# A two-layer decoder trunk on one core: the first 512 tokens of the second projection are normed and turned in the mixing phase's sample part, with two chunk buffers and key-value products per head

## The reference, cut to what matters

```python
for l in range(DEPTH):                                   # 2 layers
    mod = silu(c) @ w_ada[l] + b_ada[l]                  # conditioning: 1024 -> 3072
    shift, scale, gate = split(mod, 3)
    h = rms_norm(x, g_pre[l]) * (1 + scale) + shift
    y = mixer_ab(h) if l == 0 else mixer_c(h)            # projection in, mixing, projection out
    x = x + gate * rms_norm(y, g_post[l])
# in mixer_ab, per chunk and head (8 heads, key width 64, value width 128):
#   o = (q k^T, masked) v + q S ;  S = S * decay + k^T v
```

## Time and profile before

| | us |
|---|---|
| median of 3 runs | 2918.32 |
| lowest, highest | 2914.44, 2925.43 |
| time of the profiled execution | 2930.07 |
| its span, first to last instruction | 2928.3 |
| mean granted TensorE clock | 0.934 of full speed |

### The profile page before, as it was taken

The page is one execution under the profiler, slowest core; times in us unless marked ns, Lnnn a source line. Parts: engine busy times, 40 slices in busy tenths (PEclk is TensorE's granted clock), DMA queues, the critical chain, the costliest instruction groups (busy, mean ns, idle before and its releaser), DMA issues. The chain is left out here.

```text
span 2928.3 us, 54792 instructions
## 1 busy us (share of the span) xinstructions
PE 2645.6 (90%) x21216; PEld 1572.3 (54%) x21280; DVE 1386.1 (47%) x3146; ACT 932.6 (32%) x2711; POOL 768.8 (26%) x844
## 2 busy tenths in 40 slices
PE   7989999997599999398899999984899999999997
PEld 2434444444456653244444444453788887878783
DVE  3221212110477744486262644633566656666635
ACT  2532222222111110343131321213454554545431
POOL 1430101000311100254000010001655656465531
PEclk9999999998799988699999999997899999999977
DMA  7350212012564432355121111115431323222212
GB/s 261 112 150 31 87 37 76 29 69 78 164 220 143 143 123 68 95 164 147 38 72 54 62 58 48 51 43 129 136 89 59 97 61 94 74 81 79 62 37 72
DMA packets 264259, 270.28 MB, mean 92 GB/s; under 512 B 32126, under 2 KB 199438, under 8 KB 264015
## 3 DMA queue, kind: packets, MB, share of 16 engines
q1 hardware_dynamic: 185948, 219.50, 23.1%
q10 hardware_dynamic: 78112, 47.87, 6.1%
HBM read 179.96 MB, written 87.36 MB: 91 GB/s over the span
## 5 line engine op out<-in xcount | busy, mean ns | idle before, releaser
L518 PE MATMUL inc_b<-inc_h,inc_w_hi 128*128 128x512 bf16 (+2 forms) x1906 | 481.2, 347 | 30.1 <-DVE inc_h L462 17.2
L518 PE MATMUL inab_b<-inab_wt,inab_h 128*128 128x512 f16 (+1 forms) x1632 | 362.0, 385 | 13.0 <-POOL inab_wt L498 13.0
L518 PE MATMUL inc_b<-inc_h,inc_w_lo 128*128 128x512 bf16 (+1 forms) x926 | 301.9, 345 | 0.0
L518 PEld LDWEIGHTS inc_b<-inc_h,inc_w_hi 128*128 128x128 f16 x1920 | 170.6, 100 | 210.9 <-DVE inc_h L462 16.3
L518 PEld LDWEIGHTS inab_b<-inab_wt,inab_h 128*128 128x128 bf16 (+3 forms) x1632 | 162.6, 100 | 210.6 <-issue 26.5
L518 PE MATMUL inab_b<-inab_h,inab_wc_hi 128*128 128x512 f16 (+4 forms) x712 | 183.3, 352 | 10.7 <-DVE inab_h L462 8.0
L518 PE MATMUL inc_b<-inc_w_hi,inc_h 128*128 128x512 f16 (+3 forms) x816 | 176.4, 314 | 15.0 <-POOL inc_w_lo L498 14.3
L1777 DVE SCALAR_TENSOR_TENSOR inc_acc<-inc_ub,inc_taps,inc_acc 128x512 f32<-128x512 f32 (+1 forms) x240 | 167.5, 698 | 8.6
L1692 ACT ACTIVATE inc_ub<-inc_b 128x512 f32<-128x512 f32 x96 | 57.3, 597 | 313.1 <-PE inc_b L518 309.0
L518 PEld LDWEIGHTS inc_b<-inc_h,inc_w_lo 128*128 128x128 f16 x960 | 94.3, 100 | 93.2 <-issue 4.4
L768 ACT ACTIVATE inab_vz<-inab_b 128x512 f32<-128x512 f32 (+1 forms) x68 | 40.6, 597 | 289.6 <-PE inab_b L518 286.2
(11 more groups left out here) (415 smaller groups left out, 5534.9 us busy)
## 6 DMA issues: line engine op xcount, KB each, us to landing
tmp_qkv<-inc_so SPq DMA_DIRECT2D x96, 256.0 KB, 2.0
mixc_qkv<-tmp_qkv SPq DMA_DIRECT2D x15, 1536.0 KB, 7.7
inc_stage<-in_w_in_c ACTq DMA_DIRECT2D x32, 512.0 KB, 4.6
inab_wt<-in_w_ada SPq DMA_DIRECT2D x6, 2048.0 KB, 10.7
inab_stage<-in_w_in_ab ACTq DMA_DIRECT2D x24, 512.0 KB, 4.1
mixab_cw<-in_w_ada ACTq DMA_DIRECT2D x6, 2048.0 KB, 9.3
inab_x<-in_x_prompt SPq DMA_DIRECT2D x16, 512.0 KB, 4.7
tmp_v<-inab_vz SPq DMA_DIRECT2D x32, 256.0 KB, 3.6
```

The costliest lines, as they stand in the source:

```text
L518: last = nc.tensor.matmul(dst, lhs(a, k), rhs(b, k), start=(k == 0 and i == 0), stop=(k == KT - 1 and i == len(PASSES) - 1))
```

## The change

What is changed: (a) in mix_ab `key_values` makes one product for each head, with 64 columns of keys, so that the result lies in one bank, `kv1`, as DVE wants it; `update` is one addition; `turn_k` waits for `ktok_ready` in place of `state_ready`, and `key_values` waits for `state_ready`. The sample's products are made in the same way, into two banks. (b) `Cond` has two chunk buffers in this phase in place of three. (c) A new class `Early` loads, squares, norms, turns and stores (into `raw_next`, which lives through both phases) the first four tiles of x in the sample part. (d) Phase in_c leaves its `Prep` work for block 0 out, and uses `first_low`, `first_high` and `first_rest`, which wait for nothing of the conditioning; ACT's copy of the taps comes behind `first_low`, and the lower parts of the first weights go from DVE to POOL.

```diff
 class Cond: ... RING = 3  ->  self.ring = len(w); in mix_ab two buffers
+class Early:
+    def load(self, eng, t):
+        wait(eng, self.xnd, t)
+        eng.dma_start(self.x, self.src[t * P:(t + 1) * P, :]).then_inc(self.x_in, 16)
+    def square(self, act, t):
+        act.wait_ge(self.x_in, 16 * (t + 1))
+        wait(act, self.tr, t)
+        act.activation(self.xn, self.x, ACT.Square, accum_out=self.ss[:, t:t + 1]).then_inc(self.sq, 1)
+    def rstd(self, pool, t):                    # two operations on POOL, as in Prep
+    def norm(self, act, t):
+        act.wait_ge(self.rsd, t + 1)
+        act.activation(self.xn, self.x, ACT.Copy, scale=self.rs[:, t:t + 1]).then_inc(self.xnd, 1)
+    def turn(self, pe, t):
+        pe.wait_ge(self.xnd, t + 1)
+        wait(pe, self.done, t)
+        for k in range(KT):                     # 8 transposes into banks be, bo
+            last = self.nc.tensor.transpose(...)
+        last.then_inc(self.tr, 1)
+    def take(self, act, t):
+        act.wait_ge(self.tr, t + 1)
+        for i in range(2):
+            last = act.activation(self.raw[:, 4 * i:4 * i + 4, t * P:(t + 1) * P], self.banks[i]..., ACT.Copy)
+        last.then_inc(self.done, 1)
 phase_mix_ab, ACT:
-        for n in range(Cond.RING):
+        for n in range(2):
             cond.load(act, n)
...
-        cond.load(act, 3)
+        cond.load(act, 2)
...
         ktok_copy(nt, NS)
-        cond.load(act, 4)
+        early.load(act, 0)
+        cond.load(act, 3)
...
+        cond.load(act, 4)
+        early.square(act, 0)
+        oT_copy(nt, NS)
         cond.load(act, 5)
-        oT_copy(nt, NS)
+        def first_tile(t):
+            if t:
+                early.square(act, t)
+            early.norm(act, t)
+            if t + 1 < TPB:
+                early.load(act, t + 1)
+            early.take(act, t)
+        first_tile(0)
+        first_tile(1)
         cond.take(act)
         cond.gates(act)
+        first_tile(2)
+        first_tile(3)
 phase_mix_ab, DVE:
-            for e in range(2):
-                rows = slice(e * DKA, (e + 1) * DKA)
-                for i in range(2):
-                    kv = kvbank[i][:].rearrange("p (g e d) -> p g e d", g=2, e=2)[rows, :, e, :]
-                    last = dve.tensor_tensor(U[rows, 2 * i:2 * i + 2, :], S1[rows, 2 * i:2 * i + 2, :], kv, ALU.add)
-            chain.link(last)
+            chain.link(dve.tensor_tensor(U[:], S1[:], kv1[:].rearrange("p (g d) -> p g d", g=PAIRS), ALU.add))
 phase_mix_ab, PE:
-            wait(pe, state_ready, t)                  # turn_k
+            wait(pe, ktok_ready, t)
...
             pe.wait_ge(ktok_ready, t + 1)             # key_values
+            wait(pe, state_ready, t)
             for p in range(PAIRS):
-                last = nc.tensor.matmul(kvbank[p // 2][:, (p % 2) * 256:(p % 2 + 1) * 256], ktok[:, p, :],
-                                        v[par][:, 2 * p:2 * p + 2, :], start=True, stop=True)
+                for e in range(2):
+                    rows = slice(e * DKA, (e + 1) * DKA)
+                    last = nc.tensor.matmul(kv1[rows, p * DV:(p + 1) * DV], ktok[:, p, rows], v[par][:, 2 * p + e, :], start=True, stop=True)
...
             if p == 2:
                 cond.turn(pe)
                 cond.spread_gates(pe)
+            early.turn(pe, p)
 phase_in_c:
-        for t in range(2):
-            prep.load(sp, t, t, P)
+        prep.first_tiles_done(sp)
...
+        weights.hi(act, 0)
+        prep.first_low(act, None, m_a, m_v, first_hi)
         act.wait_ge(taps_turned, 1)
...
-        for t in range(TPB):
-            prep.norm(dve, t, t % 2, P)
-            prep.modulate_high(dve, t)
-            weights.lo(dve, t)
-        prep.copy(dve, TPB, mm, 0, BLK)
+        prep.first_high(dve, None, m_v, first_hi, first_lo_p, first_lo_v)
```

More of the change, by code:

```diff
@@ L204, in __init__ @@
         self.ident, self.sel, self.sel_s = ident, sel, sel_s
-        self.psM, self.psT, self.psG = psM, psT, psG
+        self.psM, self.psT, self.psG, self.ring = psM, psT, psG, len(w)
         s = ph.sem
-        self.w_in = [s(f"c_w_in{i}") for i in range(self.RING)]
+        self.w_in = [s(f"c_w_in{i}") for i in range(self.ring)]
         self.small_in, self.mm, self.chain, self.mod_ready = s("c_small_in"), s("c_mm"), s("c_chain"), s("c_mod_ready")
@@ L582, in phase_in_ab @@
     c9, c_silu = vz_flat[0:C9, 0:D], vz_flat[0:C9, D:2 * D]
[L583 removed]
+    ring = [w_room[:, i * 4096:(i + 1) * 4096].rearrange("p (k n) -> p k n", k=KT) for i in range(3)]
     cond = Cond(nc, ph, 0, io, modT, ring, w_room[0:C9, 12288:12288 + 3 * D], w_room[0:C9, 15360:15360 + D], r_flat[0:C9, 0:D],
@@ L1069, in phase_mix_ab @@
     cT_in, vm_ready = s("cT_in"), s("vm_ready")
-    ring = [ph.sb(f"cw{i}", [P, KT, 512]) for i in range(Cond.RING)]
+    ring = [ph.sb(f"cw{i}", [P, KT, 512]) for i in range(2)]
+    exn = ph.sb("exn", [P, D])
     mod = ph.sb("mod", [C9, 3 * D])
@@ L1182, in _ @@
         rstd(nt, NS)
+        for t in range(TPB):
+            early.rstd(pool, t)
         fin.rstd(pool, nt, NS)
@@ L1374, in _ @@
             dve.wait_ge(kv_done, nt + p + 1)
-            sv = [kv0, kv1, b_even, b_odd]
-            for i in range(4):
-                for e in range(2):
-                    rows = slice(e * DKA, (e + 1) * DKA)
-                    kv = sv[i][:].rearrange("p (s e d) -> p s e d", s=2, e=2)[rows, :, e, :]
-                    last = dve.tensor_tensor(Ss[p][rows, 2 * i:2 * i + 2, :], Ss[p][rows, 2 * i:2 * i + 2, :], kv, ALU.add)
+            for i, kv in enumerate((kv0, kv1)):
+                part = Ss[p][:, 4 * i:4 * i + 4, :]
+                last = dve.tensor_tensor(part, part, kv[:].rearrange("p (s d) -> p s d", s=4), ALU.add)
             chain.link(last)
@@ L1504, in _ @@
             pe.wait_ge(state_ready, nt + p)
-            sv = [kv0, kv1, b_even, b_odd]
-            for i in range(4):
-                last = nc.tensor.matmul(sv[i][:], ktok[0:NS, p, :], vm[p % 2][:, 2 * i:2 * i + 2, :], start=True, stop=True)
+            for i, kv in enumerate((kv0, kv1)):
+                for e in range(2):
+                    rows = slice(e * DKA, (e + 1) * DKA)
+                    last = nc.tensor.matmul(kv[rows, :], ktok[0:NS, p, rows], vm[p % 2][:, 4 * i:4 * i + 4, e * DV:(e + 1) * DV], start=True, stop=True)
             last.then_inc(kv_done, 1)
@@ L1584, in _ @@
         sp.dma_start(alog[:, 1, :], io["dt_bias_c"].unsqueeze(0).to_broadcast([P, H])).then_inc(small_in, 16)
-        for t in range(TPB):
-            sp.wait_ge(prep.xnd, t + 1)
-            prep.load(sp, t + 2, t % 2, P)
+        for t in range(TPB, TPB + 2):
+            prep.load(sp, t, t % 2, P)
         for i in range(2):
@@ L1637, in _ @@
         pool.wait_ge(prep.half_set, 1)
-        for t in range(TPB):
-            if t == 0:
-                prep.rstd(pool, 0, 0, P)
-            if t + 1 < TPB:
-                prep.rstd(pool, t + 1, (t + 1) % 2, P)
-            prep.split_lo(pool, t, t * P, P)
-        pool.wait_ge(weights.lo_done, AHEAD)
+        weights.lo(pool, 0)
+        prep.first_rest(pool, first_hi, first_lo_p)
+        for u in range(1, AHEAD):
+            weights.lo(pool, u)
         for g in range(G):
@@ L1667, in _ @@
         last.then_inc(taps_ready, 1)
-        for t in range(TPB):
-            if t == 0:
-                prep.first_square(act, 0)
-            if t + 1 < TPB:
-                prep.first_square(act, t + 1)
-            prep.modulate_low(act, t)
-            prep.split_hi(act, t, t + 1, t * P, P, 0)
-            weights.hi(act, t)
+        for u in range(1, AHEAD):
+            weights.hi(act, u)
         act.wait_ge(zero, 1)
@@ L1831, in _ @@
         pe.wait_ge(taps_ready, 1)
-        for t in range(TPB):
-            prep.turn(pe, t, P)
         seen = set()
```

53 lines of the change are left out of this document (38 added, 15 removed).

## The result

| | before | changed |
|---|---|---|
| median, us | 2921.88 (4 runs) | 2884.32 (4 runs) |
| lowest, highest | 2914.44, 2927.62 | 2880.74, 2890.29 |
| span of the profiled execution | 2928.3 | 2879.0 |

(Three of the four runs of before are those shown ahead of the prediction.) The ratio of the changed kernel to the kernel before is 0.9878, with a 95% interval of 0.9848 to 0.9908: about 36 us less. The prediction was 2869.3 us, 15 us lower.

The account below looks back on a forecast made before the run. PE, busy nine tenths of the span, bounds the kernel, so its gaps and needless work count. Terms -34.5 (in_c start), -18 (tile loop), +3.5 (sample part) sum to -49.0: median 2918.32 to 2869.3 us, range 2857 to 2886.

Parts of the forecast that it names:

- Start of in_c: Phase in_c: block 0's serial chain goes, so the first product starts at 1194.1, not 1228.66; 34.5 us less.
- rival B: Late transfers: sample-part chunk 8 to 15 us, or weight units hold in_c's first products by 5; 2877 to 2884; chance 0.18.
- I price this at nothing: Start of in_c: one weight unit ready instead of four costs nothing; some 5 us if units came late.
- Tile loop: mix_ab: shorter key-value products and no state wait cut the period from 18.35 to 17.34 us; 18 us less in all.
- Rivals A: Key-value products: column halves don't overlap; 4.3 us less loop gain, 6.6 us more in sample part; 2880; chance 0.15.
- C: Key-value products: each pass holds the array alone, weight load uncovered; total about 2920, no change; with the like, chance 0.05.
- if the stall stayed, it would be 14: mix_ab loop: gain of 14 us, not 18, if the 3.8 us stall at tiles 3 and 4 remained.
- Two chunk buffers: mix_ab: conditioning chunk n waits for chunk n-2; priced at 0, or 15 us with the slowest landing.
- Sample part: mix_ab's sample part: early x work outweighs shorter key-value products, so the sample's projection starts 3.5 us later.
- rival D: PE's granted clock stays low longer because of gaps in the sample part; +6 us, 2875; chance 0.12.
- the gap ahead of L1066: Sample part, sign of the forecast: PE stands idle ahead of L1066 for x tiles 2 and 3.
- the three that would have made the account wrong: Single-file `128*64` products at over 0.2 us; L231 waiting for `mixab_cw`; L518's product waiting for `inc_w_lo` in first four products.

Follow-up runs that it names:

- Experiment 1: Changed kernel, but ACT gives the signal for in_c's first product ahead of the upper parts of weight units 1 to 3; 2875.89 us, ratio 0.9843 to before.
- experiment 3: Changed kernel, but the loop's key transposes (`turn_k`) wait for `state_ready` again, as in the kernel before; 2885.39 us, one run.
- experiment 2: Kernel before with the per-head key-value products alone (loop and sample part), three chunk buffers, no early x work; 2903.40 us, ratio 0.9944.
- experiment 4: Changed kernel, but conditioning chunk 1 is loaded at tile 9 of the loop, not right behind chunk 0 at tile 3; 2881.04 us, ratio 0.9857 to before.
- sample order: Changed kernel, but ACT squares and norms x tile 2 ahead of `cond.take` and the gates; 2876.47 us, ratio 0.9846 to before.
- h first: Changed kernel with Experiment 1's edit, and weight unit 0 converted in the middle of making h, not ahead; 2872.18 us, ratio 0.9836 to before.
- all: Changed kernel with early signal, h first, chunks apart, sample order, and first half waiting only for the first gate operation; 2861.23 us, ratio 0.9796 to before.

## Why the prediction came out as it did

**Start of in_c: the step that failed.** "So h is ready at 1178.89 + 4.5 + 1.04 + 9.65 = 1194.1, and the first product starts there rather than at 1228.66." The first half is right, 15.2 us against 14.5. The second supposed that PE waits for h and its weights alone. PE's first product also waits for `evac`, which says that its bank is free; at the phase's start no bank is in use, and ACT gives the signal once for all of them. It gave it behind `weights.hi` of units 1 to 3. In the kernel before this cost nothing, as the same units were converted while h was made; now h overtakes them. Experiment 1 moved this signal, with the one given beside it, and nothing else, and in_c took 7.3 us less; missing were 34.5 - 27.6 = 6.9. That the weights might be late (rival B's second half) was the right place with the wrong wait: not PE's need of the units, but a signal queued behind them. That the measured 2884 us lie at the edge of B's 2877 to 2884 is luck. "I price this at nothing" is right for the units themselves: the first products never waited for them.

**Tile loop: right in the mechanism, 3 us too much.** The period was forecast at 17.34 us and is 17.25; the sixteen narrow products at 1.0 and are 1.09; the wait went to `mixab_y` as said. Rivals A and C are out: the column halves do run beside each other. One sentence of the working is wrong, though the sum did not use it: "DVE's shorter `update` moves nothing by itself". It looked at the norm behind `update` alone, but the state is written ahead of the norm and released PE's key transposes; with this wait kept, the shorter `update` was worth 0.84 us a tile (experiment 3). What was wrong in the sum is "which supposes that with two chunk loads in place of three (4 MB of traffic, not 6) the 3.8 us stall is gone". It is still 4.5 us, and between 3.8 and 4.8 in all traces with two chunks behind each other. Two things worked against each other, and experiment 2 tells them apart. With three chunks the stall was 3.8 us at turns of 18.35 us and 6.5 at turns of 17.26, which leave the tile's loads less time (one trace each); the third chunk's going brought 6.5 back to 4.5. Only pulling the chunks apart took it away (experiment 4). Nor is the stall all waiting: 1.6 of the 4.5 us are the next turn at a lower granted clock. The loop from tile 3 to 15 gained 12.4 us in place of 15.9, the turns at its two ends 2.5 in place of 2; 2.1 of the 2.5 stand ahead of tile 3, in the stretch that scatters by 3 us. The other named bound, "if the stall stayed, it would be 14", is near the 14.9 measured.

**Two chunk buffers** cost nothing, as priced: PE never waited for `mixab_cw`.

**Sample part: right in sign, 1.9 us too dear.** The groups of key-value products save 1.8 us each at the higher clock (from the first product of a group to what follows it 3.63 us before, 1.86 now) and 3.6 at the lower, as forecast; the eight transposes of a tile of x cost 1.0 us at the higher and 1.9 at the lower clock. ACT's chain for tile 2, from the last gate copy to PE's turn, took 1127.13 - 1123.84 = 3.3 us (3.35 forecast). PE came to `cond.turn` 4.6 us earlier and not 3.3, of which the gates took 0.8 back at the lower clock, and tile 3 came 0.9 us sooner, since its x landed in 3.5 us and not 4.5. From the projection to the store it took 16.8 us, 17.0 before: rival D's longer low clock did not show there, and the 1.9 us become 1.6 at the store.

**The sum** was -49.0 and is -40.5 in the traces: in_c +6.9, loop +3.1, sample part -1.9, and 0.4 over the phase ends and mix_c. Of the 15.0 us between the forecast median and the measured one, these terms are 8.5; 3.6 are the median of before, 2921.88 with its fourth run and not 2918.32; the last 2.9 are within the spread of either kernel's runs. Of the signs that were named, the one for in_c (a first product after 15 to 17 us; it came after 21.3) and the one for tiles 3 and 4 (no long tile) did not come; the period, the wait moved to `mixab_y` and the gap ahead of L1066 did, and none of the three that would have made the account wrong.

## What to carry to other kernels

When the work ahead of an engine's first instruction is cut short, list every semaphore that this instruction waits for, also those that are true at that moment and are only announced once; then look what stands ahead of each announcement in its engine's list. A signal that stood behind slow work for free becomes the bound as soon as the work beside it gets faster, and moving three lines is enough.

When a loop is made faster, price the stall from a burst of transfers anew: the loads of a tile have less time to land in a shorter turn. Here that took the stall from 3.8 to 6.5 us, and making the burst a third smaller only brought it back to 4.5. What counts is whether the next tile's own loads, the last and smallest among them, still land before PE needs them; spreading the burst over turns took the stall away whole.

Before saying which engine made a loop shorter, follow the chain that closes on itself from one turn to the next, and compare it step by step. PE's products and DVE's addition both got shorter here, and only one of them was on the chain that the state closes.

## What the runs showed of the hardware

Phase in_ab has the same instructions in all ten kernels, and it ends at either 711.6 to 713.6 us (changed, key-values alone, sample order, h first, all) or 719.2 to 721.6 us (the other five). In the first five PE's granted clock is 1.00 between 300 and 500 us, in the other five 0.97; 3% of 200 us are 6 us. The window in the kernel before (its clock is the third value from the end):

```profile
300.00:500.00 200.00, 194.94 (x878) 89.65 (x883) 43.70 (x53) 55.95 (x95) 27.53 (x18) 0.97 0.20 70
```

And in the changed kernel:

```profile
300.00:500.00 200.00, 195.48 (x911) 90.50 (x910) 43.94 (x53) 58.00 (x98) 27.64 (x18) 1.00 0.19 68
```

So six to ten microseconds of a single execution's time come and go in a phase that no edit touches, most of it together with the granted clock (each kernel has one trace, so why an execution has the one or the other is not shown). This is as much as most of the edits here bring, and is why they were read by the length of their own phase.

Two products on the two column halves of the array over all 128 rows, of which the trace before had none, run beside each other: sixteen of 128 columns took 1.09 us, and eight of 256 columns, as many columns in all, took 1.99. This agrees with the Trainium skill, "TensorEngine Tiling (Array Packing)", section Overview, which gives up to 2x for stationary blocks of at most 64 columns. Measured is 1.8x.

In three traces a wait of PE in the tile loop was paid twice. Behind the 2.7 us that it waited at tile 4 of the changed kernel, the granted clock of the next turn was 0.91 in place of 1.00, and this turn took 1.6 us longer. In the kernel before and in experiment 2 the turn behind the wait has 0.91 too, and takes 1.7 and 1.6 us longer.
